# Rebuilt opening, closing and scratch round trip of a two-block fp32 network on one core

## What is computed

```python
def rmsnorm(x, gain):
    y = x * rsqrt(mean(x * x, -1) + 1e-6); return y * gain

def swiglu(h, w_in, w_out):
    gate, up = split(h @ w_in, 2); return (silu(gate) * up) @ w_out

for l in range(2):                                  # first block
    x = x + 0.5 * swiglu(rmsnorm(x, ffn1_norm[l]), ffn1_w_in[l], ffn1_w_out[l])
    x = x + hybrid_mixer(rmsnorm(x, mix_norm[l]), ...)
    x = x + 0.5 * swiglu(rmsnorm(x, ffn2_norm[l]), ...)
...                                                 # second block: same frame, other mixer
return rmsnorm(x, final_norm)
```

## Time and profile before

| what | us |
|---|---|
| median of 3 runs | 2798.99 |
| lowest and highest | 2796.64, 2799.72 |
| profiled execution, its own time | 2799.07 |
| its span | 2797.3 |
| PE busy | 2737.7 (98%) |
| DVE busy | 1575.1 (56%) |
| ACT busy | 1388.1 (50%) |
| POOL busy | 116.8 (4%) |
| granted clock of TensorE, mean | 0.995 |

### The profile page before, as it was taken

One profiled execution on the slowest core, in us unless ns is written; L12 is line 12 of the kernel. 1 busy time (PEld: TensorE's weight loads), 2 busy tenths in 40 slices (PEclk: granted clock), 3 DMA queues, 4 the chain that ended last, 5 costly groups with the idle time before them and its releaser, 6 DMA issues.

```text
span 2797.3 us, 40834 instructions
## 1 busy us (share of the span) xinstructions
PE 2737.7 (98%) x16612; PEld 2413.0 (86%) x16612; DVE 1575.1 (56%) x1694; ACT 1388.1 (50%) x1522; POOL 116.8 (4%) x146
## 2 busy tenths in 40 slices
PE   6999999999999999999999999999999999999999
PEld 5889999988888899998888889888888889888887
DVE  4447854664544586556445555556545545555654
ACT  4445774454544467545445445445445445544543
POOL 0000170000000005200000000000000000000000
PEclk9999999999999999999999999999999999999999
DMA  6556445465565454545555555435655565433653
GB/s 204 193 174 184 157 136 175 145 203 191 182 191 194 144 166 153 167 140 186 194 189 185 190 179 165 136 93 166 201 187 193 184 195 158 128 121 121 206 192 127
DMA packets 396950, 475.15 MB, mean 170 GB/s; under 512 B 26950, under 2 KB 365198, under 8 KB 396558
## 3 DMA queue, kind: packets, MB, share of 16 engines
q1 hardware_dynamic: 391776, 470.79, 52.9%
q10 hardware_dynamic: 5038, 2.40, 0.3%
HBM read 467.51 MB, written 5.64 MB: 169 GB/s over the span
## 4 chain that ended last, share of the span: by engine, by line
PE 85%; DVE 4%; POOLq 4%; issue 2%; ACT 2%; DMA 1%; DVEq 1%; SPq 0%; POOL 0%; ACTq 0%
PE bank L322 26%; PE bank L324 25%; PE bank L323 25%; POOLq L1762 2%; POOLq L1759 2%; DVE w_lo L317 1%; PE bank L637 1%; PE bank L1911 1%; DVE conv_acc L1531 1%; PE bank L1889 1%; PE bank L1197 1%; PE bank L443 1%; DMA inv_t<-inv_t_scratch 1%; PE bank L1899 1%; DMA raw<-in_ffn_w_in 1%
## 5 line engine op out<-in xcount | busy, mean ns | idle before, releaser
L730 DVE TENSOR_TENSOR w_lo<-raw,w_hi 128x2048 fp32r<-128x2048 f32 x240 | 550.2, 2293 | 532.2 <-ACT w_hi L701 532.2
L322 PE MATMUL bank<-w_hi,xn_hi 128*128 128x512 f32 (+2 forms) x2208 | 796.9, 361 | 8.1 <-DVE xn_lo L423 7.4
L324 PE MATMUL bank<-w_hi,xn_lo 128*128 128x512 f32 (+2 forms) x2208 | 789.9, 358 | 0.0
L323 PE MATMUL bank<-w_lo,xn_hi 128*128 128x512 f32 (+2 forms) x2208 | 789.8, 358 | 0.0
L701 ACT ACTIVATE w_hi<-raw 128x2048 fp32r<-128x2048 f32 x240 | 459.4, 1914 | 409.6 <-PE bank L324 409.6
L317 DVE TENSOR_TENSOR w_lo<-raw,w_hi 128x2048 fp32r<-128x2048 f32 (+1 forms) x202 | 444.0, 2201 | 233.6 <-ACT w_hi L311 233.3
L322 PEld LDWEIGHTS bank<-w_hi,xn_hi 128*128 128x128 f32 x2208 | 418.9, 190 | 70.7 <-issue 6.4
L324 PEld LDWEIGHTS bank<-w_hi,xn_lo 128*128 128x128 f32 x2208 | 419.0, 190 | 60.6
L323 PEld LDWEIGHTS bank<-w_lo,xn_hi 128*128 128x128 f32 x2208 | 419.2, 190 | 59.7 <-issue 0.5
L311 ACT ACTIVATE w_hi<-raw 128x2048 fp32r<-128x2048 f32 (+1 forms) x202 | 369.5, 1831 | 85.0 <-PE bank L324 71.1
L322 PE MATMUL bank<-xn_hi,w_hi 128*128 128x256 f32 (+1 forms) x1392 | 407.0, 292 | 2.3 <-ACT ba_rows L1321 1.2
(11 more groups left out here) (319 smaller groups left out, 2678.8 us busy)
## 6 DMA issues: line engine op xcount, KB each, us to landing
raw<-in_w_in SPq DMA_DIRECT2D x126, 1024.0 KB, 5.3
raw<-in_ffn_w_in SPq DMA_DIRECT2D x176, 512.0 KB, 4.7
raw<-in_ffn_w_out SPq DMA_DIRECT2D x44, 1024.0 KB, 4.9
raw<-in_ffn_w_gate SPq DMA_DIRECT2D x88, 512.0 KB, 4.0
raw<-in_ffn_w_up SPq DMA_DIRECT2D x88, 512.0 KB, 5.0
raw<-in_ffn_w_down SPq DMA_DIRECT2D x44, 1024.0 KB, 4.9
raw<-in_w_out SPq DMA_DIRECT2D x10, 1024.0 KB, 5.0
raw<-in_w_branch_b SPq DMA_DIRECT2D x8, 1024.0 KB, 9.5
```

The lines of the kernel that those rows point to most:

```text
L322: pe.matmul(out, a_hi, b_hi, start=start, stop=False, skip_group_check=check)
L323: pe.matmul(out, a_hi, b_lo, start=False, stop=False, skip_group_check=check)
L324: return pe.matmul(out, a_lo, b_hi, start=False, stop=stop, skip_group_check=check)
L730: dve.tensor_tensor(w_lo[slot][:, :], raw[slot][:, :], w_hi[slot][:, :].bitcast(F32), ALU.subtract).then_inc(s_lo, 1)
```

## The change

Four things are rebuilt. (1) Opening: SP brings only the identity, then the left half of x, the gain, the first item in two halves (row groups 0 and 1, then 2 and 3), the right half of x, and then the other items. DVE multiplies and splits x first; item 0 is split in halves by both engines, and PE begins with the first half. ACT loads its table by a dummy copy. Three dummy products on zeros give the first signals of `s_used`. (2) The small parameters are brought by SP behind the first FFN's weights; PE and DVE turn and copy the vectors on the way into the first mixer. `dt_alog` is laid out so that each partition has one piece of 64 bytes per vector. (3) `store_inverses` stores `Xd` after the first signal and `XdT` after the second, and `Ti` and `Ui` have semaphores of their own; `XdT` moves to other bytes. (4) Closing: x is multiplied by the gain chunk by chunk behind each update, squares are taken by chunk, and the last scaling is shared: ACT takes the left half of each tile, DVE the right. ACT issues one of the four stores.

```diff
@@ -388,6 +393,11 @@
+        def bring_x(sp, n):
+            sp.dma_start(x[:, :, half(n)], a["x"].rearrange("b (t p) d -> p (b t) d", p=P)[:, :, half(n)]
+                         ).then_inc(s_xhalf[n], 16)
@@ -407,8 +417,8 @@
-            if c == 0:
-                dve.wait_ge(s_const, 32)
+            if c % 2 == 0:
+                dve.wait_ge(s_xhalf[c // 2], 16)
@@ -461,12 +471,54 @@
-            pe.wait_ge(s_const, 32)
+            pe.wait_ge(s_const, 16)
...
+        def first_rows(t, h):
+            return t[0][:, 1024 * h:1024 * h + 1024]
+        def first_ffn_act(act, p):
+            high_act(act, 0, 0, BY_HALVES)
+            act.wait_ge(s_first, 32)
+            act.wait_ge(s_used, p.freed(0))
+            act.activation(first_rows(w_hi, 0), first_rows(raw, 0), ACT.Copy).then_inc(s_first_hi, 1)
+            high_act(act, 0, 1, BY_HALVES)
+            act.wait_ge(loaded[0], p.loaded(0))
+            act.activation(first_rows(w_hi, 1), first_rows(raw, 1), ACT.Copy).then_inc(s_hi, 1)
+            square_act(act, 0, 0, 3)
+            square_act(act, 0, 1, 4)
+            split_hi(act, p, 1)
+            high_act(act, 0, 2, BY_HALVES)
+            high_act(act, 0, 3, BY_HALVES)
...
+        def first_ffn_dve(dve, p, update):
+            def low(h, ready, count, done):
+                dve.wait_ge(ready, count)
+                dve.tensor_tensor(first_rows(w_lo, h), first_rows(raw, h), first_rows(w_hi, h).bitcast(F32),
+                                  ALU.subtract).then_inc(done, 1)
+            for c in range(2):
+                update(dve, 0, c, BY_HALVES)
+                gain_dve(dve, 0, c, BY_HALVES)
+            low_dve(dve, 0, 0, BY_HALVES)
+            low(0, s_first_hi, 1, s_first_lo)
+            low(1, s_hi, p.base + 1, s_lo)
+            for c in range(2, 4):
+                update(dve, 0, c, BY_HALVES)
+                gain_dve(dve, 0, c, BY_HALVES)
+            low_dve(dve, 0, 1, BY_HALVES)
+            split_lo(dve, p, 1)
+            low_dve(dve, 0, 2, BY_HALVES)
+            low_dve(dve, 0, 3, BY_HALVES)
...
@@ -513,8 +565,24 @@
+            if q == 1:
+                turn_vecs_pe(pe)
...
+        def turn_vecs_pe(pe):
+            pe.wait_ge(s_gains, 16 * n_gains)
+            for b in range(4):
+                n = ROWS1 if b < 2 else ROWS2
+                mm = pe.transpose(bank[7][:, P * b:P * b + n], vrows[0:n, b, :], ident[0:n, 0:n])
+            mm.then_inc(s_vT, 1)
+        def vecs_dve(dve):
+            dve.wait_ge(s_vT, 1)
+            for b in range(4):
+                n = ROWS1 if b < 2 else ROWS2
+                ins = dve.tensor_copy(vecs[b // 2][:, b % 2, 0:n], bank[7][:, P * b:P * b + n])
+            ins.then_inc(s_vecs, 1)
@@ -593,7 +663,14 @@
-            gate_up(0, 0, 0, 0)
+            if f == 0:
+                dst = raw[0][:, :].rearrange("p (k s n) -> p k s n", k=4, s=2)
+                for k, signal in ((slice(0, 2), s_first), (slice(2, 4), loaded[0])):
+                    sp.dma_start(dst[:, k, 0, :], cols(gate_w, gate_at)[:, k, :]).then_inc(signal, 16)
+                    sp.dma_start(dst[:, k, 1, :], cols(up_w, up_at)[:, k, :]).then_inc(signal, 16)
+                bring_x(sp, 1)
+            else:
+                gate_up(0, 0, 0, 0)
@@ -614,6 +693,8 @@
+                    if early and first and h == 0 and t == 0 and k == 2:
+                        pe.wait_ge(s_lo, p.base + (j + 1 + START))
@@ -622,7 +703,10 @@
-                pe.wait_ge(s_lo, p.base + (j + 1 + START))
+                if early and first and h == 0:
+                    pe.wait_ge(s_first_lo, 1)
+                else:
+                    pe.wait_ge(s_lo, p.base + (j + 1 + START))
@@ -835,7 +919,7 @@
-        XdT = put("diag_inverse_t", [32, 32], at=early)
+        XdT = put("diag_inverse_t", [32, 32], at=early + 8192)
@@ -1002,20 +1088,22 @@
+            sp.wait_ge(s_zero, 32)
+            sp.wait_ge(s_solve, l * 2 + 1)
+            for b in range(3):
+                s, x_ = slice(32 * b, 32 * b + 32), slice(16 * b, 16 * b + 16)
+                at = 32 * (b % 2)
+                sp.dma_start(t_dram[s, :, at:at + 32].rearrange("i s j -> s i j"), Xd[x_, :, :]).then_inc(s_ind, 16)
...
-            sp.wait_ge(s_zero, 32)
...
-                if b < 3:
-                    at = 32 * (b % 2)
-                    sp.dma_start(t_dram[s, :, at:at + 32].rearrange("i s j -> s i j"),
-                                 Xd[x_, :, :]).then_inc(s_ind, 16)
-                sp.dma_start(u_dram[s, :, s].rearrange("j s i -> s j i"), XdT[x_, :, :]).then_inc(s_ind, 16)
+                sp.dma_start(u_dram[s, :, s].rearrange("j s i -> s j i"), XdT[x_, :, :]).then_inc(s_indt, 16)
...
-            sp.wait_ge(s_ind, 112 * l + 112)
+            sp.wait_ge(s_ind, 48 * l + 48)
...
-            sp.dma_start(Ui[:, :, :, :].rearrange("p c h n -> p (c h) n"), u_dram).then_inc(s_inv, 16)
+            sp.wait_ge(s_indt, 64 * l + 64)
+            sp.dma_start(Ui[:, :, :, :].rearrange("p c h n -> p (c h) n"), u_dram).then_inc(s_invt, 16)
@@ -1197,7 +1285,7 @@
-                pe.wait_ge(s_inv, 32 * l + 32)
+                pe.wait_ge(s_inv, 16 * l + 16)
@@ -1206,6 +1294,7 @@
+                pe.wait_ge(s_invt, 16 * l + 16)
@@ -2235,31 +2324,48 @@
+        def store_y(engine, c):
+            t, n = BY_ROWS[c]
+            engine.dma_start(out_dram.rearrange("b (t p) d -> p (b t) d", p=P)[:, t, half(n)],
+                             xg[:, c, :]).then_inc(s_stored, 16)
+        def bring_small(sp):
+            for b in (0, 1):
+                at = 0
+                for name, n in vec_rows[b]:
+                    sp.dma_start(vrows[at:at + n, 2 * b:2 * b + 2, :],
+                                 W[name].rearrange("l (k p) -> k l p", p=P)).then_inc(s_gains, 16)
+                    at += n
+                if b == 0:
+                    sp.dma_start(vrows[at:at + 96, 0:2, :],
+                                 W["dn_conv_w"].rearrange("l j (k p) -> (j k) l p", p=P)).then_inc(s_gains, 16)
+            rest = slice(P, where["causal"][0])
+            sp.dma_start(consts[:, rest], consts_dram[:, rest]).then_inc(s_rest, 16)
+            for i, name in enumerate(("dn_dt_bias", "dn_a_log")):
+                sp.dma_start(dta[:, i, :, :], W[name].partition_broadcast(P)).then_inc(s_rest, 16)
...
-            sp.dma_start(consts[:, 0:2 * P], consts_dram[:, 0:2 * P]).then_inc(s_const, 16)
-            sp.dma_start(x[:, :, :], W["x"].rearrange("b (t p) d -> p (b t) d", p=P)).then_inc(s_const, 16)
+            sp.dma_start(consts[:, 0:P], consts_dram[:, 0:P]).then_inc(s_const, 16)
+            bring_x(sp, 0)
...
+                if (b, l) == (0, 0):
+                    bring_small(sp)
...
-            for c, (t, n) in enumerate(BY_ROWS):
-                sp.wait_ge(s_y, c + 1)
-                sp.dma_start(out_dram.rearrange("b (t p) d -> p (b t) d", p=P)[:, t, half(n)],
-                             xg[:, c, :]).then_inc(s_stored, 16)
+            for c, signal, count in ((0, s_yact, 1), (1, s_y, 1), (3, s_y, 2)):
+                sp.wait_ge(signal, count)
+                store_y(sp, c)
...
-            pe.wait_ge(s_const, 32)
-            pe.wait_ge(s_gains, 16 * n_gains)
-            for b in range(4):
-                n = ROWS1 if b < 2 else ROWS2
-                pe.transpose(bank[7][:, P * b:P * b + n], vrows[0:n, b, :],
-                             ident[0:n, 0:n]).then_inc(s_used if b < START else s_vT, 1)
+            for i in range(START):
+                pe.matmul(bank[7][:, 0:P], zeros[:, :], zeros[:, :], start=True, stop=True).then_inc(s_used, 1)
@@ -2277,32 +2383,35 @@
-            for b in (0, 1):
...
-            for i, name in enumerate(("dn_dt_bias", "dn_a_log")):
-                act.dma_start(dta[:, :, i, :], W[name].partition_broadcast(P)).then_inc(s_rest, 16)
-            rest = slice(2 * P, where["causal"][0])
-            act.dma_start(consts[:, rest], consts_dram[:, rest]).then_inc(s_rest, 16)
...
+            act.activation(warm[:, :], eps_col[:, 0:1], ACT.Copy)
...
-                    to_ffn_act(act, q, p)
+                    if q == 0:
+                        first_ffn_act(act, p)
+                    else:
+                        to_ffn_act(act, q, p)
...
-            for t in range(NT):
-                square_act(act, last_norm, t, 2 * t + 2)
-                root_act(act, slice(t, t + 1))
+            def scaled_act(t):
+                act.wait_ge(s_xg, 4 * last_norm + (2 * t + 1))
+                act.wait_ge(s_rstd, LAYERS * 2 * 2 + t + 1)
+                act.activation(xg[:, 2 * t, :], xg[:, 2 * t, :], ACT.Copy, scale=rstd[:, t:t + 1]).then_inc(s_yact, 1)
+            act.activation(warm[:, :], eps_col[:, 0:1], ACT.Sqrt)
+            chunk_square_act(act, last_norm, 0)
+            chunk_square_act(act, last_norm, 1)
+            token_root_act(act, last_norm, 0)
+            chunk_square_act(act, last_norm, 2)
+            scaled_act(0)
+            chunk_square_act(act, last_norm, 3)
```

(32 more changed lines are left out.)

47 lines of the change are left out of this document (26 added, 21 removed).

## The result

The changed kernel took 2775.01 us (median of 4 runs, 2774.64 to 2776.45), the kernel before, beside it on the same chip, 2798.34 us: ratio 0.9918, 95% interval 0.9901 to 0.9935. Run again it took 2772.69 (6 runs) against 2796.25, ratio 0.9925 (0.9913 to 0.9937). The sign was right, the forecast was wrong.

A forecast was written before the change was run, and what follows sets the result against it. TensorE, busy nearly the whole span, was taken as the bound, so only its standstills or the end could be won: opening 13.7, inverses 3.3, closing 0, together 17.0 us off 2799.07, forecast 2782 us, range 2779 to 2788.

The forecast's parts named there:

- Opening, 13.7 us: Start of the kernel: first product at 12.55 instead of 26.55 us, 14.0 less a 0.25 us wait for item 1.
- low end: Whole kernel, 2779 us: landings 1 us sooner, five fewer slow products and the best closing, 3.1 us in all.
- Small parameters behind the first FFN, nothing: Nine transfers moved behind the first FFN's weights: no cost, 7.7 us of cover remaining before the mixer's first item.
- Inverses, 3.3 us: Delta steps of the first block's two layers: PE's waits for inv_t go, 2.2 and 1.1 us.
- The bound of 3.4: Delta steps: upper limit of the gain from removing the inv_t waits; the lower limit was 2.5 us.
- Closing, 0: End of the kernel: net nothing, fourth update 1.0 us late; bounds 1.1 us faster and 0.6 us slower.
- 2799.07 - 17.0 = 2782.1: Whole kernel: time of the profiled execution before, less the summed gains, giving the predicted 2782 us.
- soft spot: Opening: number of slow first products, taken as eleven; six would give another 1.0 us, sixteen would cost 1.0.
- A: Opening: slow stretch from 8 to 13 us stays, not of the small rows' making; 2784.4 us; chance 0.10.
- B: Middle: removing the inverse waits wins nothing, as something else holds the delta step; 2785.4 us; chance 0.05.
- C: First mixer: small rows in SP's queue block the ring before the mixer's weights; slower, 2822 us; chance 0.02.

The follow-up runs named there:

- e3: Kernel before with only the rebuilt opening and the small parameters brought later; 2784.06 us, ratio 0.9957.
- e1: Kernel before with only the inverses change: stores in two parts, own semaphores for Ti and Ui; 2787.85 us, ratio 0.9979.
- e2: Kernel before with only the new closing; 2795.88 us, ratio 1.0005.
- e4: Kernel before with one added memset of 1024 columns on VectorE ahead of the first x_gained; 2799.57 us, ratio 1.0010.
- e9: Kernel before with only a semaphore of its own for Ui, awaited at delta step 1; 2790.66 us, ratio 0.9975.
- e11: Changed kernel without the inverses change (stores, loads and one wait as before); 2782.99 us, ratio 0.9944.
- e14: Changed kernel with dummy products at the mixers' entries and the fourth x update ahead of the first tile's scaling; 2773.26 us, ratio 0.9920.
- e5: Changed kernel without any edit, timed again beside the kernel before; 2772.69 us, ratio 0.9925.
- e8: Kernel before with only the two dt_alog transfers moved behind the first FFN's weights; 2791.57 us, ratio 0.9985.
- e13: Changed kernel with one scaling done twice at each of the four mixers' entries, lengthening PE's pauses; 2781.08 us, ratio 0.9943.
- e12: Changed kernel with dummy products of zeros in PE's pauses at the mixers' entries; 2772.74 us, ratio 0.9917.

## Why the prediction was wrong

- **Opening, 13.7 us**: right, a little small. 14.3 us between the two traces, 14.5 of work in e3. The working held step by step: gain at 6.98 for 7.6, first product at 11.81 for 12.55, eleven slow products, a short wait for item 1. The landings came some 0.7 us sooner, which the low end had allowed for ("landings 1 us sooner"). The shift between the traces contains the slow landing of item 0 in the profile of before, some 0.8 us that e1, e2, e4 and e9 do not have. The rate held too (311 to 367 GB/s from 3 to 18 us).
- **Small parameters behind the first FFN, nothing**: right. ACT's first split waits for PE.
- **Inverses, 3.3 us**: right in mechanism, a little small: 2.4 + 1.3 between the traces, 3.3 (e9), 4.1 (e1) and 4 (e11) in the runs. The bound of 3.4 was tight, because it took both waits from one profile: e11's came to 4.7, those of e3 to 3.0.
- **Closing, 0**: right (e2 +0.5, traces 0.05), with the fourth update late as said. Another order of it does not win the late update's 0.8 us back (e14).
- **The step that failed**: the sum itself, by a term put at nothing. "2799.07 - 17.0 = 2782.1" took over the clock of one profiled run for the new kernel, in a trace whose page gave its mean as 0.995, and neither sum nor range had a term for it. Work makes 18.3 to 18.8 us, 1.5 more than the sum, inside what the range allowed; the rest of the 23.3, some 5 us (6 between the two profiles), is clock. About 3 us of that go with the waits for `inv_t`, by the two groups of kernels with and without them. The other part, some 2 us, cannot be told from chance: the four first runs of before, at a median of 2798.34, were slower than its mean over the 80 runs beside the experiments, 2796.4, and in e5, where the difference was 23.6 us again, the six runs of the changed kernel had a clock of 0.9982 against 0.9976 for their group.
- **The rivals**: A is refuted by e8, B by e1 and e9; of C there is no trace. There should have been a fourth, on the other side of the forecast: that a pause removed returns more than its length (e13 shows the reverse of it).
- **The "soft spot"**: mis-costed. Both first profiles have eleven slow products, and the term was right for that number. But "six would give another 1.0 us", and with it a microsecond of the low end, does not fit the prediction's own working, in which item 1 is ready only at 21.3, by the work of ACT and DVE. The profile of e5, the same kernel, has seven slow products, and PE only waits longer for item 1:

```profile
20.82 0.47 PE L327 MATMUL bank<-w_hi,xn_hi 128*128 128x512 f32 x1 [0.88 <-DVE xn_lo L433]
```

With eleven item 1 begins at 20.72, with the twelve of e13 and e14 at 21.2: fewer give nothing, and one more costs 0.4 us. The Trainium skill (TensorE: Matmul & The Clock Gate, Part 1) has the number of slow products change between runs; the traces agree (seven to twelve).

**What stays open.** Why the falls come at these few places and not elsewhere, why they hit in some runs and not in others, and why the one at the entry of the second mixer (near 942 us), far from any wait for `inv_t`, is also rarer in kernels without that wait (in the profiles five of six against one of seven). That pauses matter is shown in one direction only: longer ones lower the clock (e13), shorter ones at the mixers show no gain (e12).

## What to carry to other kernels

In a kernel whose PE is 98% busy, count the stretches of lower clock in the trace before making the sum: they are a term of their own, and a pause of PE that is removed may give back more than its length. Keep transfers in hundreds of pieces of 32 bytes out of the time in which the first tiles are awaited, also when they are on another queue. When two tiles share a semaphore, ask which is wanted first; either splitting the semaphore or issuing the pair earlier can be enough alone.

## What was unexpected in the hardware

- Two transfers of 16 KB in all, in 512 pieces of 32 bytes on ACT's queue, came with a rate of 105 GB/s over both queues for 5 us, at 39% busy DMA engines; without them it was 382.
- The granted clock falls to its lower level in the midst of a kernel whose PE is 98% busy, zero to nine times in the profiles here, mostly at the same few places of the program, and differently in executions of the same instructions. Each fall costs about 1.5 us, and the time of a run follows its mean clock by 2.4 us for each 0.001.
- Four stores of 256 KB issued within 0.9 us took 3.7 us from the last issue to the end, the same four spread over 2.5 us took 2.9 (one profile of the first kind).
